# First half's low parts behind the second half's chain at three norms; the last product by token halves, its input's order changed; the output in four pieces

## The reference

```python
# blocks 1 and 2: after each sublayer (8 times; norm 0 to norm 7 in the kernel)
x = layer_norm(alpha * x + sublayer(x), g, b)      # mean and variance over the 1024 columns
# block 3, its end
merged = g_m[..., :D_MODEL] * (y_a @ w_branch_a) + g_m[..., D_MODEL:] * (y_b @ w_branch_b)
x = x + merged @ w_out
```

## Time and profile before

| | |
|---|---|
| median of 3 runs | 2755.16 us (2754.97 to 2759.5) |
| the profiled execution's own time | 2762.04 us |
| its span in the profile | 2759.9 us |
| PE busy | 2634.3 us (95%) |
| DVE busy | 1944.2 us (70%) |
| ACT busy | 1528.4 us (55%) |
| mean granted TensorE clock | 0.975 of full |

### The profile page before, as it was taken

How to read it: one execution, slowest core, us unless ns; L and a number is a source line. 1 busy time by engine, 2 the same in 40 slices (tenths; PEclk the granted TensorE clock), 3 DMA queues, 4 the chain that set the end, 5 groups by cost and what they waited for, 6 DMA issues and landing times.

```text
span 2759.9 us, 34405 instructions
## 1 busy us (share of the span) xinstructions
PE 2634.3 (95%) x14799; PEld 2276.5 (82%) x14799; DVE 1944.2 (70%) x1940; ACT 1528.4 (55%) x1602; POOL 50.7 (2%) x38
## 2 busy tenths in 40 slices
PE   8999989998999998999979999999999999979998
PEld 7999877796998977998967888888888888867886
DVE  4557679565555665546658898898989898976854
ACT  4446445443444353444647777777777777755752
POOL 0000000000001000001000000000000000010000
PEclk9999989999999999999988999999999999989999
DMA  6545333453555544585338999999999999955332
GB/s 250 185 177 191 138 122 123 140 197 107 183 183 204 192 142 145 191 226 192 115 115 333 347 358 345 338 356 346 361 344 358 347 358 346 358 225 192 138 122 78
DMA packets 88639, 632.27 MB, mean 229 GB/s; under 512 B 9792, under 2 KB 9808, under 8 KB 13472
## 3 DMA queue, kind: packets, MB, share of 16 engines
q1 hardware_dynamic: 84496, 610.24, 60.1%
q0 software_dynamic: 3984, 19.76, 2.6%
HBM read 625.77 MB, written 4.19 MB: 228 GB/s over the span
## 4 chain that ended last, share of the span: by engine, by line
PE 85%; DVE 10%; ACT 3%; DMA 1%; issue 1%; DVEq 0%; POOL 0%; SPq 0%; ACTq 0%; POOLq 0%
PE pw L716 14%; PE pw L717 14%; PE pw L718 14%; PE py L716 12%; PE py L717 11%; PE py L718 11%; DVE lo L698 3%; ACT hi L695 1%; DMA raw<-in_wts 1%; PE pw L2494 1%; DVE XL L910 1%; PE pw L2431 1%; PE pw L2432 1%; PE pw L897 1%; PE pw L872 1%
## 5 line engine op out<-in xcount | busy, mean ns | idle before, releaser
L698 DVE TENSOR_TENSOR lo<-raw,hi 128x2048 fp32r<-128x2048 f32 x406 | 925.8, 2282 | 392.5 <-ACT hi L695 392.1
L695 ACT ACTIVATE hi<-raw 128x2048 fp32r<-128x2048 f32 x414 | 785.9, 1900 | 405.0 <-PE py L718 325.6
L716 PE MATMUL pw<-XH,hi 128*128 128x256 f32 x1688 | 486.1, 288 | 14.5 <-DVE lo L698 5.4
L717 PE MATMUL pw<-XL,hi 128*128 128x256 f32 x1688 | 483.4, 286 | 0.0
L718 PE MATMUL pw<-XH,lo 128*128 128x256 f32 x1688 | 483.2, 286 | 0.0
L698 DVE TENSOR_TENSOR lo<-raw,hix 128x2048 fp32r<-128x2048 f32 x168 | 384.9, 2292 | 53.5 <-ACT hix L695 50.3
L717 PE MATMUL pw<-lo,GH 128*128 128x512 f32 x896 | 354.4, 396 | 0.0
L716 PEld LDWEIGHTS pw<-XH,hi 128*128 128x128 f32 x1688 | 330.0, 195 | 20.4 <-DVE lo L698 6.5
L695 ACT ACTIVATE hix<-raw 128x2048 fp32r<-128x2048 f32 x168 | 321.7, 1916 | 39.1 <-PE py L718 37.5
L717 PEld LDWEIGHTS pw<-XL,hi 128*128 128x128 f32 x1688 | 330.1, 196 | 1.1
L718 PEld LDWEIGHTS pw<-XH,lo 128*128 128x128 f32 x1688 | 329.9, 195 | 0.0
(11 more groups left out here) (514 smaller groups left out, 3819.7 us busy)
## 6 DMA issues: line engine op xcount, KB each, us to landing
raw<-in_wts SPq DMA_DIRECT2D x577, 1024.0 KB, 4.8
GB<-in_rows POOLq DMA_DIRECT2D x8, 1024.0 KB, 5.0
scratch_bias<-dr POOLq DMA_DIRECT2D x1, 3072.0 KB, 35.8
BI<-scratch_bias POOLq DMA_DIRECT2D x1, 2048.0 KB, 11.9
raw<-in_wts SPq DMA_DIRECT2D x3, 512.0 KB, 3.2
raw<-in_wts SPq DMA_DIRECT2D x2, 576.0 KB, 3.6
X<-in_x SPq DMA_DIRECT2D x1, 1024.0 KB, 5.4
nrow<-in_rows POOLq DMA_DIRECT2D x2, 512.0 KB, 4.6
```

Source lines behind the costliest of these rows:

```text
L695: L.e.activation(hi, raw, ACT.Copy).then_inc(*L.up("hi", n))
L698: L.e.tensor_tensor(lo, raw, f32(hi), ALU.subtract).then_inc(*L.up("lo", n))
L716: T_.e.matmul(o, x[0], w[0], start=first, stop=False)
L717: T_.e.matmul(o, x[0], w[1], start=False, stop=False)
```

## The change

- **Three norms.** In `residual`, for norms 2, 4 and 6 DVE's two low parts of half 0 (`dve_turn_half(..., 0)`) stand behind the whole chain of half 1 (statistics to scaling) instead of ahead of it. For norms 0, 3 and 5 they stay.
- **The end of block 3.** The last two tiles of `bb` run without the owed splits; both splits come after them. The low parts of both halves of `m3` come after both halves of `bb`.
- **o3** waits for half 0 of `m3` only before its matmuls of half 0, and for half 1 before those of half 1; its last two tiles are joined (`ahead=True`). `ready` now takes `tt`.
- **The output** goes out in four DMAs of 128 x 512, each after its own addition.

```diff
+TILES3 = [n for n in range(E1, len(SEQ)) if SEQ[n][0] != "o3"]
...
-                                    for point in ready(kx) if callable(ready) else ready:
+                                    for point in ready(kx, tt) if callable(ready) else ready:
...
+            by_half = j in (0, 3, 5)
...
-                if ends:
+                if ends and by_half:
                     dve_turn_half(L, ("x", j), XH, XL, 0)
                 for h in range(2):
                     dve_stats(L, dst, 1, h)
                 dve_centre(L, j, dst, 1)
                 dve_scale(L, j, 1)
+                if ends and not by_half:
+                    dve_turn_half(L, ("x", j), XH, XL, 0)
                 if ends:
                     dve_turn_half(L, ("x", j), XH, XL, 1)
...
-            if h == 1 and L.kind == "A":
-                act_turn_half(L, "m3", XH, tt)
-            if h == 1 and L.kind == "V":
-                dve_turn_half(L, "m3", XH, XL, tt)
+            if h == 1 and tt == 1:
+                for q in range(2):
+                    if L.kind == "A":
+                        act_turn_half(L, "m3", XH, q)
+                    else:
+                        dve_turn_half(L, "m3", XH, XL, q)
...
-            run(pe_tm(T_, "o3", XP, 8, D, D, [turned_half("m3", 1)]))
+            run(pe_tm(T_, "o3", XP, 8, D, D, lambda kx, tt: [turned_half("m3", tt)], True))
...
-            weave(tiles3(V), dve_side3(V), lambda: refill(V, None, True))
+            tiles = tiles3(V)
+            weave(islice(tiles, len(TILES3) - 2), dve_side3(V), lambda: refill(V, None, True))
+            run(tiles)
+            refill(V, None, True)
...
-            S.wait_ge("ev", ("o3", 0, 1, 1))
-            S.e.dma_start(out.rearrange("a (t p) n -> p (a t) n", p=P), X[:, :, :]).then_inc(sem_out, 16)
-            S.e.wait_ge(sem_out, 16)
+            rows = out.rearrange("a (t p) n -> p (a t) n", p=P)
+            for tt in range(2):
+                for h in range(2):
+                    s = slice(h * 512, (h + 1) * 512)
+                    S.wait_ge("ev", ("o3", 0, tt, h))
+                    S.e.dma_start(rows[:, tt, s], X[:, tt, s]).then_inc(sem_out, 16)
+            S.e.wait_ge(sem_out, 64)
```

More of the change, by code:

```diff
@@ L2087, in tiles_sb @@
                 yield from pe_tm(L, "svb", XP, 8, 512, 512, x_of(5))
-                yield from pe_tm(L, "so", (DH, DL), 8, D, D, lambda kx: [turned(("sot", kx // 2), 2)], True)
+                yield from pe_tm(L, "so", (DH, DL), 8, D, D, lambda kx, tt: [turned(("sot", kx // 2), 2)], True)
             else:
@@ L3371, in tensor @@
             run(side)
-            weave(pe_tm(T_, "ro", (RH, RL), 16, D, D, lambda kx: [turned(("gg", kx // 4), 4)], True),
+            weave(pe_tm(T_, "ro", (RH, RL), 16, D, D, lambda kx, tt: [turned(("gg", kx // 4), 4)], True),
                   after(2, pe_feat, T_, 3))
```

## The result

| | before | after |
|---|---|---|
| median of 10 runs each | 2756.27 (2754.47 to 2759.5) | 2748.56 (2745.99 to 2751.39) |
| profiled execution, its own time | 2762.04 | 2748.1 |
| its span | 2759.9 | 2746.0 |
| granted clock, mean | 0.975 | 0.978 |

The ratio is 0.9968, 95% interval 0.9960 to 0.9976: faster by 6.6 to 11.0 us. The forecast was 13.15 us and 2742.0, the range ended at 2747.0. The sign was right, the size was not.

The account below looks back on a forecast made before the run. PE's matmuls (85% of the chain) set the time, DVE counting only where PE stands still. 4.55 + 3.95 + 2.7 + 1.95 = 13.15 us off the 2755.16 median gave 2742.0 us, range 2742.0 - 4.5 to 2747.

Parts of the forecast that it names:

- o3's start, 3.95: End of block 3: o3 starts at 2723.0 instead of 2726.95, 3.95 us earlier; bounds 1.4 and 4.3.
- The clock, 2.7: In o3: the clock stays up, so its steps take 21.7 us instead of 24.39, saving 2.7; bounds 0 and 2.7.
- The norms, 4.55: Norms 2, 4, 6: statistics start 1.48, 1.59 and 1.48 us earlier, together 4.55; bounds 0 and 4.8.
- a PE that never waits there passes an earlier start on unchanged: Experts' stage, PE busy 100 of 100 us at full clock: savings ahead of it should reach the end.
- the norms give nothing, the pair is again in the way: Norms 2, 4, 6: moved low parts delay PE again, or the next product waits for splits; 2746.6 us, chance 0.07.
- The output, 1.95: Kernel's end: last 256 KB piece lands after 2.55 us instead of 4.5 for 1 MB, saving 1.95; bounds 0 and 2.1.
- the third piece, 1.4 us ahead, is near: Output: pieces 1 to 3 leave up to 8 us ahead, only the third near the last; no cost was taken.
- The base: Starting median 2755.16 us; the profiled execution was 6.9 over the median, the same difference assumed after the change.
- The range: Whole kernel: 2742.0 - 4.5 up to 2747, to hold 8 in 10, including clock and output at their worst together (2746.6).
- The clock did not fall at the end: Answers the case that the clock falls at o3 anyway, losing the 2.7 us: 2744.7 us, chance 0.13.
- No low part came late: Answers the case that low parts of o3.1 or o3.3 come late in o3: 2744 us, chance 0.05.
- The output's DMAs overlap: Answers the case of four output DMAs running one after another: 2750.7 us at 4.5 each, 2760.7 at 7; chance 0.03.

Follow-up runs that it names:

- e7: Kernel before with eleven thrown-away matmuls between m3's two sets of transposes; ratio 0.9989 [0.9979, 0.9999], mean -3.2 us against before, 11 runs.
- e12: Changed kernel, 18 thrown-away matmuls each at norms 2, 4, 6, plus 24 at the router's wait and 48 at norm 7; ratio 0.9927 to before, 2738.1 us.
- e5: The changed kernel once more, nothing altered; mean -6.7 us against before, ratio 0.9974, 12 runs.
- e6: Changed kernel without the norms' new order (new end of block 3 and four output DMAs only); mean -6.9 us against before, ratio 0.9969.
- e3: Kernel before with only the output cut into four DMAs; mean +0.5 us against before, ratio 1.0002.
- e13: Changed kernel with its output in one DMA as before; mean -6.8 us against before, ratio 0.9976.
- e14: Changed kernel with output in one DMA and 18 thrown-away matmuls at each of norms 2, 4, 6; mean -18.9 us against before, ratio 0.9939.
- e16: Changed kernel with 18 thrown-away matmuls at each of norms 2, 4, 6; mean -22.0 us against before, ratio 0.9924.
- e15: Changed kernel with the norms' old order and 25 thrown-away matmuls at each of norms 2, 4, 6; mean -11.0 us against before, ratio 0.9964.

## Why the prediction was wrong

**By its own steps.** All timed runs but those of e7 and e12 (237 with those of before) can be fitted by least squares with a level for each chip's session and one term for each part. The last column has these terms with their 95% intervals; "in the traces" is what the stretch where the part acts got shorter, mean against mean:

| | forecast | in the traces | in the times |
|---|---|---|---|
| norms | 4.55 | 3.7, filled 4.53 | 1.6 +- 1.1 |
| o3's start and the clock | 3.95 + 2.7 | 4.04 + 2.6 | 5.9 +- 1.1 |
| output | 1.95 | 1.5 | 0.2 +- 1.0 |
| sum | 13.15 | 11.8 | 7.7 |

The fit has two terms more: filling the norms' waits gives 4.6 +- 1.5, and the norms' order in filled kernels 8.7 +- 1.9 on top of its 1.6. It takes the norms and the end as independent. With one more term for the two together, the norms alone are 3.1 +- 1.6 and the end alone 6.5 +- 1.2, and where both are in the kernel 2.7 +- 2.3 of that are lost. So the shortfall may lie in the adding up as much as in a single part.

- *o3's start, 3.95*: right. From matmul 14600 to o3's first is 26.91 in every trace with the old end and 22.87 or 22.88 in every one with the new: 4.04.
- *The clock, 2.7*: right, o3 takes 21.66 or 21.67 against 24.11 to 24.43 in the unfilled ends.
- *The norms, 4.55*: **this is the step that failed**, by its premise in the first paragraph: "a PE that never waits there passes an earlier start on unchanged". The prediction itself wrote that it expected the clock to fall at the norms as before, and yet passed the gain through this fall at its full size. Where the product starts 1.5 us earlier and the clock rises when it did, those 1.5 us are spent at half speed. In the means of the traces that takes 0.6 at norm 2, 0.3 at norm 4 and nothing at norm 6. That this is the clock, and not the rival "the norms give nothing, the pair is again in the way", is shown by the kernels that differ in the filling alone: there the three terms are whole. What becomes of the remaining 3.7 farther on is less clear. The short wait near 1036 us (matmuls 6200 to 6460) took 64.5 us in the mean of the six traces with the old order and 65.4 in that of the four with the new; but this stretch takes 63.5, 65 or 66 in either order where the norms are filled, and from matmul 6700 to 8692 the means differ by 0.4 the other way. Over the whole way from matmul 4060 to 8900 the old order took 809.9 to 813.8, mean 812.4, the new one 809.1 to 809.3, mean 809.2: 3.2 us. In times the norms give 1.6 +- 1.1, and beside the new end (e5 and e6) nothing. So of the 2.95 us that the term is short, the traces show about 1.4, of which 0.9 at the norms are the clock's; where the other 1.6 go is open.
- *The output, 1.95*: mis-sized, the second step that failed. The prediction noted that the third piece, 1.4 us ahead, is near, and put that at nothing. In the changed kernel the last piece is issued at 2740.01, when the third has not landed yet, and lands at 2743.23. Over the ten traces with four pieces the last one lands 2.5 to 3.4 us after its issue, 2.9 in the mean, against 4.4 to 4.5 for the one DMA (2.55 against 4.5 in the sum). From the start of the last matmul to the span's end it is 6.82 in the mean with four pieces and 8.36 with one: 1.5 saved. That the nearness of the third piece is the reason was not tested. Own time less span is 2.0 to 2.2 in every profiled execution, so nothing is given back there. In times e3 shows +0.5, e13 against e5 0, e14 against e16 3.1: in the fit 0.2 +- 1.0. Why the times fall short of the traces' 1.5 stays open.
- *The base.* The profiled execution of before was an odd one: 2762.04, above all but five of the 93 timed runs of the kernel before that stood beside the experiments (2750.56 to 2762.94). The pair of profiled spans, 13.9 apart, was not a measurement of the sum: it holds 2.7 and 1.5 us at two places that come and go in one and the same kernel (matmuls 2400 to 2700 took 56.2 before, 53.5 after, and 56.4 in e5, the same kernel as after; and the place near 1036 us), less 1.1 and 1.7 at two others. And the median of before was 2756.27 beside the changed kernel, 1.1 above the one that the forecast started from.
- *The range.* It held the unknown terms at their worst, but no case in which a term is right where it arises and shrinks behind it. With 3.2 for the norms the traces' sum is 11.3: from 2756.27 that makes 2745.0. The 3.6 us from there to 2748.56 are traces against times and are not explained.

**Against the rivals.** The clock did not fall at the end. No low part came late: o3's 96 matmuls have no wait among them. The output's DMAs overlap: the last is issued before the third has landed. By the Trainium skill (DMA: Bandwidth & Descriptors, Anatomy of one DMA), 2.0 us fixed plus the bytes over 436e9 per second, 256 KB take an estimated 2.6 us; the last piece of the changed kernel took 3.2, and 2.5 to 3.4 in the ten traces, so the measurement decides.

**Left open.** The 4 us between the traces' sum (11.8, or 11.3 with 3.2 for the norms) and the times (7.7). The difference falls on all three parts, most on the norms (3.7 against 1.6) and the output (1.5 against 0.2). One profile per kernel may not sample the falls of the clock as its 5 to 12 timed runs do; that the profiled executions differ otherwise can't be excluded. Whether block 3's clock can be kept up by design was not tried; e12, which filled the waits at the router and at norm 7, lost it (112.30 in that stretch).

## What to carry to other kernels

Ask of every gain whether the tensor engine's clock falls behind it. Here a start brought forward by 4.5 us into stretches at half clock gave 3.7 there in the traces, and 1.6 in the times; the one brought forward by 4.0 with no fall behind it passed in full. A wait of 4 to 6 us in a chain of matmuls costs more than its length, and matmuls whose result is thrown away, ended just before the wait does, are a cheap cure. At the three norms, 75 of them shortened the old order's stretches by 6.9 us (4.8 in the times), 54 the new order's by 7.9. The times gave 13.5 for the latter, but some 4.8 of that hang on block 3's clock, which may not stay up elsewhere. And where a program has many short waits, compare stretches between the same two instructions over several traces of one kernel before reading a difference of two spans; here two traces agreed with a wrong sum.

## What the runs showed of the hardware

- The spread of one kernel's runs goes with the clock. In 93 runs of the kernel before the mean granted clock runs from 0.974 to 0.980, and the mean time falls as it rises: 2761.2 us at 0.974, 2759.2 at 0.976, 2757.0 at 0.978, 2754.7 at 0.980.
- A difference between two kernels can be larger than what was removed: the norms' order removes 4.5 us, and e15 and e16 differ by 11.3, of which 5.6 are at the norms and 4.8 in a stretch of block 3 that has the same instructions in both, where the granted clock fell in one and stayed at 1.00 in the other. What decides on that is open.
- The clock's rise is tied neither to the start of the wait nor to the restart. In the ten traces with unfilled norms it came 12.2 to 15.6 us after PE had gone idle, and 6.4 to 9.6 us after PE had restarted with the transposes (in the kernel before 13.6, 14.0 and 15.2 after PE had gone idle, in the changed one 13.3, 12.7 and 12.6).
- Four DMAs of 256 KB in place of one of 1 MB: the last lands 2.5 to 3.4 us after its issue where it comes 1.4 us behind the third, the one DMA 4.4 to 4.5.
